# A hybrid attention layer on one core: copies of h on ScalarE, earlier sums, rotated tiles stored ahead of weights

## The chip, the cores and the metric

The kernel runs on one NeuronCore of a Trainium2 chip. The metric is the device time of one execution in microseconds (us), as the median of several executions. The engines are named as the profile names them: PE (TensorE, matrix products), PEld (its weight loads), DVE (VectorE), ACT (ScalarE), POOL (GpSimd) and SP (SyncE, which issues the DMAs here; SPq is its queue).

## What is computed

One layer over x of shape 1024 x 1024, with 256 memory tokens. What matters for the change is the start: the norm, the combined projection, and the rotary turn of queries and keys.

```python
def hybrid_layer(x, mem, g_pre, w_in, w_conv, attn_sink, g_mem, w_mem_kv,
                 w_up_a, w_up_b, w_up_m, w_out, g_post):
    h = rms_norm(x, g_pre)
    proj = h @ w_in                                   # 1024 x 1024 by 1024 x IN_WIDTH
    (a_b, a_c, a_x, a_z, b_q, b_k, b_v, b_z, m_q, m_z, gate_logits) = jnp.split(proj, idx, axis=-1)
    ua = (short_gated_conv(a_b, a_c, a_x, w_conv) * silu(a_z)) @ w_up_a
    q, k = partial_rope(b_q, pos), partial_rope(b_k, pos)
    ub = (window_attention_with_sink(q, k, b_v, attn_sink) * silu(b_z)) @ w_up_b
    mk, mv = jnp.split(rms_norm(mem, g_mem) @ w_mem_kv, 2, axis=-1)
    um = (memory_cross_attention(m_q, mk, mv) * silu(m_z)) @ w_up_m
    merged = gates[0] * ua + gates[1] * ub + gates[2] * um      # sigmoid gates of gate_logits
    return x + rms_norm(merged @ w_out, g_post)
```

## The kernel before

Every fp32 product is made of three fp32r products: each operand is split into a high part (a rounded copy) and a low part (value minus high part), and high·high, high·low and low·high are summed in PSUM. High parts are made by ACT, low parts by POOL or DVE.

The projection is worked off in pairs of 128-column tiles. Weights come in 128x512 blocks (`spots`), and each is split into a ring of four (`high_part`, L1060, on ACT; `low_part`, L657, on POOL). One entry of the ring is a "slot"; slots 0 to 11 are the four blocks A11, A21, A12, A22 of each of the first three pairs, which are multiplied directly (`first_pair` and `direct_pair`). They give the keys, the values and the four query tiles. From pair 3 (`P_DIRECT`) on, seven products by Strassen's scheme replace eight: P1, P2, P6, P7, P4, P5, P3, in that order (slots 12 to 18, then 19 to 25 for pair 4, and so on). They need four combinations of the blocks of h: T1 = B12 - B11, T3 = B22 - B12, T2 = B22 - T1, T4 = B21 - T2, each of four 128x512 pieces. P6 uses T2, P7 T3, P4 T4 and P5 T1, and each combination needs high and low parts again (`high_of_combination` on ACT; `low_of_combination` on DVE, for T1 half on DVE and half on POOL).

h itself is made in the first pair: PE transposes a piece of scaled x into PSUM (`turn_x`, L804), ACT writes the high part times g_pre (`high_of_h`), and DVE's `copy_h` (L1374) makes the low part of piece 0 and of odd pieces, and an fp32 copy of each of the 16 pieces into `area`, from which POOL takes the low parts of the even pieces (`low_of_h`, L663) and DVE the sums. PE may overwrite a PSUM bank with the piece four further on once it has been copied.

The five tiles of keys and queries ("rope tiles", 0 the keys, 1 to 4 queries) are rotated on DVE: `swap_rows` and `times_cos` read PSUM, `rotate` (two instructions, L1517 and L1519) reads SBUF alone. Then ACT writes the high part (`rope_high`, L1127), POOL the low part (`rope_low`, L676), and SP stores both to DRAM (`store_rope`, L394). `times_cos` of tiles 2 and 3 reuses the space of tiles 0 and 1 and so waits for their stores. When all five are rotated, SP copies one strip of the last (`last_queries`), loads the first attention block (`load_block(0)`, L449), and PE scores it ahead of P6 of pair 4.

All five engine programs are written out by hand, and each engine keeps that order: an instruction that waits holds everything behind it. `sums_first` (L1416) makes the first weight sums of a pair from A11, A21 and A22. SP loads A22 of pair 3 once POOL has made the low part of slot 11. These lines show the order on two of the engines:

```python
            high_of_combination(T3)      # ACT, behind high_part(7)
            high_part(8)
            high_of_combination(T2)
            high_part(9)
            rope_high(0)
            high_part(10)
            rope_high(1)
            high_part(11)
            high_of_combination(T4)
```

Of the kernel before, what the change touches and what calls it, by code (L numbers as in the profile page):

```python
# [155 lines left out]
def hybrid_layer(nc, x, mem, w8, wup, wmem, wout, g_pre, g_mem, g_post, w_conv, sink,  # L156
                 cos, sin, mask, ident_in, out):
    ctx = ExitStack()
    with ctx:
# [142 lines left out]
        x_turned, h_copied, comb_hi = sem("x_turned"), sem("h_copied"), sem("comb_hi")  # L302
# [76 lines left out]
        def _(sp):  # L379
# [52 lines left out]
            for j in range(4):  # L432
                load_spot(j, 2)
            load_spot(A11, 3)
            load_spot(A12, 3)
            store_rope(0)
            load_spot(A21, 3)
            load_spot(A22, 3)
            store_rope(1)
# [108 lines left out]
            for p, name in ORDER[N_DIRECT:]:  # L548
# [8 lines left out]
                if name == "P1":  # L557
                    load_spot(A11, p + 1)
                    if p == P_DIRECT:
                        store_rope(2)  # L560
# [12 lines left out]
                elif name == "P6":  # L573
                    load_spot(A22, p + 1)
                    store_block(p - 1, "next P6")
                    if p == P_DIRECT:
                        store_rope(3)
# [6 lines left out]
                elif name == "P7":  # L584
                    store_block(p - 1, "next P7")
                elif name == "P4":
                    if p == P_DIRECT:
                        last_queries()
                        load_block(0)
                        store_rope(4)  # L590
                    if p == P_LAST:
                        load_gate(0)
                elif name == "P5":
                    if 1 <= gr < ATT_GROUPS and gr % 2 == 1:
                        load_sb(gr // 2)
                    if P_CONV <= p < P_LAST:
                        load_mq(p + 1 - P_CONV)
# [59 lines left out]
        def _(pool):  # L657
# [5 lines left out]
            def low_of_h(n):  # L663
                idx, j, place = H_BLOCKS[n]
                pool.wait_ge(h_copied, n + 1)
# [26 lines left out]
            low_part(7)  # L692
            low_part(8)
            low_part(9)
            rope_low(0)
            low_part(10)
            rope_low(1)
            low_part(11)
            low_part(12)
            low_part(13)  # L700
# [3 lines left out]
            rope_low(2)  # L704
            low_part(15)
            low_part(16)
            low_part(17)
            low_part(18)
            rope_low(3)
            low_part(19)  # L710
            rope_low(4)
            for n in range(20, NS + 3):
                low_part(n)
# [11 lines left out]
        def _(pe):  # L725
# [25 lines left out]
            def first_pair():  # L751

                for n in range(2 * KC):
                    half, kk = divmod(n, KC)
                    for m in {5: (), 6: (8,), 7: (9, 10)}.get(n, (n + 3,)):
                        if 4 <= m < 2 * KC:
                            pe.wait_ge(h_copied, m - 3)
# [301 lines left out]
        def _(act):  # L1059
# [26 lines left out]

            def high_of_combination(idx):
# [17 lines left out]
            for n in range(2 * KC):  # L1105
                high_of_h(n)
                if n == 1:
                    square_sum(5)
# [19 lines left out]
            def rope_high(j):  # L1128
                act.wait_ge(roped, j + 1)
                if j == 0:  # L1130
                    act.wait_ge(comb_hi, 2 * HC)
# [5 lines left out]
            high_of_combination(T3)  # L1137
            high_part(8)
            high_of_combination(T2)
            high_part(9)  # L1140
            rope_high(0)
            high_part(10)
            rope_high(1)
            high_part(11)
            high_of_combination(T4)
            high_part(12)
            high_part(13)
            high_of_combination(T1)
            high_part(14)
            rope_high(2)  # L1150
# [3 lines left out]
            nc.scalar.copy(v_raw, tile_bank(V_TILE)).then_inc(v_copied, 1)  # L1154

# [70 lines left out]
            for n, (p, name) in list(enumerate(ORDER))[N_DIRECT:]:  # L1226
# [24 lines left out]
                elif name == "P2":  # L1251
                    if p - 1 in SILU:
                        block_sigmoid(p - 1, 3, c12)
                elif name == "P6":
                    if p == P_DIRECT:
                        rope_high(3)
# [4 lines left out]
                elif name == "P7":  # L1261
                    if p == P_DIRECT:
                        rope_high(4)
# [81 lines left out]
        def _(dve):  # L1345
# [29 lines left out]
            def copy_h(n):  # L1375
# [3 lines left out]
                dve.wait_ge(h_hi_made, n + 1)  # L1379
# [4 lines left out]
                nc.vector.tensor_scalar(f32(place, HALF), spare[n % 4], g, None, ALU.mult).then_inc(h_copied, 1)  # L1384

            def sum_t1(j):
                b11, b12 = f32(B11F + j * HALF, HALF), f32(B12F + j * HALF, HALF)
                dve.wait_ge(h_copied, KC + j + 1)
# [3 lines left out]
            def sum_t3(j):  # L1392
                b22, b12 = f32(B22F + j * HALF, HALF), f32(B12F + j * HALF, HALF)
                dve.wait_ge(h_copied, KC + HC + j + 1)
                nc.vector.tensor_tensor(f32(T3F + j * HALF, HALF), b22, b12, ALU.subtract).then_inc(sum_made[T3], 1)

            def sum_t2(j):
# [3 lines left out]
                if j == 0:  # L1401
                    dve.wait_ge(h_lo_pool, KC - 1)
# [122 lines left out]
            for n in range(2 * KC):  # L1525
# [5 lines left out]
                if n >= KC + HC:  # L1531
                    sum_t1(n - KC - HC)
            swap_rows(0)
            times_cos(0)
            for j in range(HC):
                sum_t3(j)
            for j in range(HC):
                sum_t2(j)
# [19 lines left out]
            rotate(3)  # L1558
            rotate(4)
# [142 lines left out]
            for p, name in ORDER[N_DIRECT:]:  # L1702
# [36 lines left out]
                elif name == "P6":  # L1739
                    add_p6(p)  # L1740
                    if p == P_DIRECT:
                        low_of_combination(T1)
# [219 lines left out]
```

## Time and profile before

| what | us |
|---|---|
| median of three runs | 941.97 |
| lowest and highest of them | 941.80, 942.54 |
| the profiled execution, whole | 942.66 |
| its span on the core | 940.8 |
| PE busy | 915.8 (97%) |
| PEld busy | 768.4 (82%) |
| DVE busy | 619.5 (66%) |
| ACT busy | 422.6 (45%) |
| POOL busy | 378.4 (40%) |

The span runs from the first to the last instruction on the core, and the whole execution is 1.9 us longer. Lines such as L660 are lines of the kernel before. The granted clock of PE is at full speed over nearly all of the span (0.999 of it on average). The page puts 97% of the span as PE busy; which of the remaining stretches can be won, and by what, is read from the waits and the timeline.

### The profile page before, as it was taken

Reading aid. Unit: us, or ns where it says so; the run is one execution under the profiler, and the core shown is the slowest. Engines: PE = TensorE matmul, PEld = TensorE weight load, DVE = VectorE, ACT = ScalarE, POOL = GpSimd, SP = SyncE. Lnnn points to the kernel's source line nnn. Section 1 sums busy time; section 2 is a strip of 40 time slices with the busy share of each in tenths; the row PEclk is TensorE's granted clock in tenths of the full one; section 3 lists DMA queues with packets and bytes.
Section 4 is the critical chain, followed back from the end, with each engine's and each line's share of the span. In section 5 each row is a group of like instructions: output and inputs, shape, how many; then the busy total and the mean of one; then the engine's idle time right before and its main releaser. Section 6 shows DMA issues by size and latency. Waiting matters only on the chain. (4 is left out here: it accounts for less than half of the span.)

```text
span 940.8 us, 12512 instructions
## 1 busy us (share of the span) xinstructions
PE 915.8 (97%) x4360; PEld 768.4 (82%) x4360; DVE 619.5 (66%) x1057; ACT 422.6 (45%) x802; POOL 378.4 (40%) x260
## 2 busy tenths in 40 slices
PE   5999999999999999999999999999999999999997
PEld 4788778888888888888888888888888888888885
DVE  5799966655556666656576278888896367763443
ACT  7434465444445466544462434343443553432211
POOL 2457834444444344444434744444442644300000
PEclk9999999999999999999999999999999999999999
DMA  7242656342424333624253422222222874641222
GB/s 281 85 119 82 168 175 204 103 157 101 157 101 160 110 118 107 194 95 171 100 173 132 146 67 80 84 83 81 79 78 85 320 234 146 224 156 68 90 90 89
DMA packets 81181, 124.43 MB, mean 132 GB/s; under 512 B 7008, under 2 KB 40416, under 8 KB 81120
## 3 DMA queue, kind: packets, MB, share of 16 engines
q1 hardware_dynamic: 81120, 123.65, 39.8%
q8 instruction: 35, 0.57, 0.2%
q14 instruction: 26, 0.21, 0.1%
HBM read 90.46 MB, written 33.55 MB: 132 GB/s over the span
## 5 line engine op out<-in xcount | busy, mean ns | idle before, releaser
L660 POOL TENSOR_TENSOR ring<-spots,ring 128x512 fp32r<-128x512 f32 x218 | 311.9, 1434 | 401.7 <-ACT ring L1063 388.9
L733 PE MATMUL pm<-hc,ring 128*128 128x512 f32 x728 | 286.7, 394 | 2.2 <-POOL ring L660 2.2
L735 PE MATMUL pm<-hc,ring 128*128 128x512 f32 x728 | 284.1, 390 | 0.0
L734 PE MATMUL pm<-hc,ring 128*128 128x512 f32 x728 | 283.7, 390 | 0.0
L1063 ACT ACTIVATE ring<-spots 128x512 fp32r<-128x512 f32 x218 | 136.6, 628 | 260.3 <-PE pm L735 183.8
L733 PEld LDWEIGHTS pm<-hc,ring 128*128 128x128 f32 x728 | 136.8, 188 | 29.3 <-issue 2.5
L735 PEld LDWEIGHTS pm<-hc,ring 128*128 128x128 f32 x728 | 136.6, 188 | 28.9
L734 PEld LDWEIGHTS pm<-hc,ring 128*128 128x128 f32 x728 | 136.8, 188 | 26.8
L1289 ACT ACTIVATE area<-area 128x1024 f32<-128x1024 f32 x24 | 25.5, 1061 | 60.6 <-DMA area<-raw_d 60.6
L1013 PE MATMUL pm<-hc,ring 128*128 128x512 f32 x128 | 49.9, 390 | 0.0
L1014 PE MATMUL pm<-hc,ring 128*128 128x512 f32 x128 | 49.8, 389 | 0.0
L1015 PE MATMUL pm<-hc,ring 128*128 128x512 f32 x128 | 49.8, 389 | 0.0
L1048 PE MATMUL pm<-hc 128*128 128x512 f32 x128 | 49.8, 389 | 0.0
L1049 PE MATMUL pm<-hc 128*128 128x512 f32 x128 | 49.8, 389 | 0.0
L1050 PE MATMUL pm<-hc 128*128 128x512 f32 x128 | 49.8, 389 | 0.0
L1460 DVE TENSOR_TENSOR snaps<-pm,snaps 128x512 f32<-128x512 f32 x26 | 17.9, 689 | 37.6 <-PE pm L735 37.6
L1612 DVE TENSOR_TENSOR area<-pv,area 64x512 f32<-64x512 f32 x16 | 11.0, 689 | 46.4 <-ACT area L1171 46.4
L1177 ACT ACTIVATE area<-area,st 128x384 f32<-128x384 f32 x64 | 38.4, 601 | 0.0
L1068 ACT COPY snaps<-pm 128x512 f32<-128x512 f32 x26 | 15.3, 589 | 48.4 <-PE pm L735 48.4
L1806 DVE TENSOR_TENSOR hc<-spots,hc 128x512 fp32r<-128x512 f32 x16 | 22.7, 1418 | 21.7 <-ACT hc L1303 21.6
L1449 DVE TENSOR_TENSOR area<-pm,snaps 128x512 f32<-128x512 f32 x26 | 18.0, 691 | 25.4 <-PE pm L735 17.4
L1184 ACT ACTIVATE area<-area,st 128x384 f32<-128x384 f32 x64 | 34.2, 606 | 0.2
(206 smaller groups left out, 1617.6 us busy)
## 6 DMA issues: line engine op xcount, KB each, us to landing
spots<-in_w SPq DMA_DIRECT2D x116, 256.0 KB, 3.0
raw_d<-area SPq DMA_DIRECT2D x72, 256.0 KB, 2.0
area<-raw_d SPq DMA_DIRECT2D x24, 512.0 KB, 3.5
area<-in_x SPq DMA_DIRECT2D x16, 512.0 KB, 4.8
spots<-in_wup SPq DMA_DIRECT2D x24, 256.0 KB, 3.9
q_d<-area_r SPq DMA_DIRECT2D x16, 256.0 KB, 4.4
area<-raw_d SPq DMA_DIRECT2D x16, 256.0 KB, 3.2
area<-in_wmem SPq DMA_DIRECT2D x16, 256.0 KB, 2.9
```

Source lines behind the costliest of these rows:

```text
L660: nc.gpsimd.tensor_tensor(ring[:, n % RING, 1, :], operand(n), ring[:, n % RING, 0, :].bitcast(F32), ALU.subtract).then_inc(lo_made, 1)
L733: pe.matmul(bank, hi, moving_hi(k), start=(k == 0), stop=False)
L734: pe.matmul(bank, hi, moving_lo(k), start=False, stop=False)
L735: mm = pe.matmul(bank, lo, moving_hi(k), start=False, stop=(k == HC - 1))
L1013: pe.matmul(dst, hi, y[:, at, 0, cols], start=(begin and c == chunks[0]), stop=False)
L1014: pe.matmul(dst, hi, y[:, at, 1, cols], start=False, stop=False)
L1015: mm = pe.matmul(dst, lo, y[:, at, 0, cols], start=False, stop=(end and c == chunks[-1]))
L1048: pe.matmul(dst, hi, wo[:, k, 0, :], start=(k == 0), stop=False)
L1049: pe.matmul(dst, lo, wo[:, k, 0, :], start=False, stop=False)
L1050: mm = pe.matmul(dst, hi, wo[:, k, 1, :], start=False, stop=(k == KC - 1))
L1063: nc.scalar.activation(ring[:, n % RING, 0, :], operand(n), ACT.Copy).then_inc(hi_made, 1)
L1177: ins = nc.scalar.activation(probs[:, h, :], probs[:, h, :], ACT.Exp, bias=st[:, 3, h:h + 1], accum_out=st[:, 5, h:h + 1])
```

## The change

In the first pair, the second eight fp32 copies of h (pieces 8 to 15) move from DVE to ACT, each right behind the piece's high part; DVE keeps their odd low parts, and waits for ACT's copy before each. DVE makes the pieces of T1 and T3 in turns from piece 13 on, then T2, and only then rotates tile 0. ACT and POOL take `rope_high` and `rope_low` of each tile further ahead among the weight blocks, ACT makes T4's high parts before `high_part(11)`, and DVE makes its half of T1's low parts between `rotate(3)` and `rotate(4)` rather than in P6 of pair 3. SP stores tile 0 ahead of the loads of A11 and A12 of pair 3, tile 1 ahead of A21 and A22, and moves the last loads and stores from P4 of pair 3 to P6. The arithmetic is the same. The diff, without the repeated context:

```diff
@@ sync: loads and stores around the direct pairs
+            store_rope(0)
             load_spot(A11, 3)
             load_spot(A12, 3)
-            store_rope(0)
+            store_rope(1)
             load_spot(A21, 3)
             load_spot(A22, 3)
-            store_rope(1)
+            store_rope(2)
...
                 if name == "P1":
                     load_spot(A11, p + 1)
                     if p == P_DIRECT:
-                        store_rope(2)
+                        store_rope(3)
...
                     load_spot(A22, p + 1)
                     store_block(p - 1, "next P6")
                     if p == P_DIRECT:
-                        store_rope(3)
+                        last_queries()
+                        load_block(0)
+                        store_rope(4)
...
                 elif name == "P4":
-                    if p == P_DIRECT:
-                        last_queries()
-                        load_block(0)
-                        store_rope(4)
@@ gpsimd
-                pool.wait_ge(h_copied, n + 1)
+                if n < KC:
+                    pool.wait_ge(h_copied, n + 1)
+                else:
+                    pool.wait_ge(h_copied_act, n - KC + 1)
...
             low_part(7)
+            rope_low(0)
             low_part(8)
             low_part(9)
-            rope_low(0)
-            low_part(10)
             rope_low(1)
-            low_part(11)
-            low_part(12)
-            low_part(13)
+            for n in range(10, 14):
+                low_part(n)
+            rope_low(2)
             for j in (0, 2):
                 low_of_combination(T1, j)
             low_part(14)
-            rope_low(2)
             low_part(15)
+            rope_low(3)
             low_part(16)
             low_part(17)
-            low_part(18)
-            rope_low(3)
-            low_part(19)
             rope_low(4)
-            for n in range(20, NS + 3):
+            for n in range(18, NS + 3):
                 low_part(n)
@@ tensor, first_pair
-                            pe.wait_ge(h_copied, m - 3)
+                            if m - 4 < KC:
+                                pe.wait_ge(h_copied, m - 3)
+                            else:
+                                pe.wait_ge(h_copied_act, m - 3 - KC)
+                                pe.wait_ge(h_lo_dve, h_lo_count(m - 4, h_lo_dve))
@@ scalar
+            def copy_h(n):
+                nc.scalar.activation(f32(H_BLOCKS[n][2], HALF), spare[n % 4], ACT.Identity,
+                                     scale=gpre[:, n % KC:n % KC + 1]).then_inc(h_copied_act, 1)
...
                 high_of_h(n)
+                if n >= KC:
+                    copy_h(n)
...
                 if j == 0:
-                    act.wait_ge(comb_hi, 2 * HC)
+                    act.wait_ge(sum_made[T2], HC)
+                    act.wait_ge(h_lo_pool, h_lo_count(2 * KC - 1, h_lo_pool))
...
             high_of_combination(T3)
+            rope_high(0)
             high_part(8)
             high_of_combination(T2)
             high_part(9)
-            rope_high(0)
+            rope_high(1)
             high_part(10)
-            rope_high(1)
+            high_of_combination(T4)
             high_part(11)
-            high_of_combination(T4)
             high_part(12)
             high_part(13)
+            rope_high(2)
             high_of_combination(T1)
             high_part(14)
-            rope_high(2)
             high_part(15)
...
             nc.scalar.copy(v_raw, tile_bank(V_TILE)).then_inc(v_copied, 1)
+            rope_high(3)
...
                 elif name == "P2":
+                    if p == P_DIRECT:
+                        rope_high(4)
...
                 elif name == "P6":
-                    if p == P_DIRECT:
-                        rope_high(3)
...
                 elif name == "P7":
-                    if p == P_DIRECT:
-                        rope_high(4)
@@ vector
-                dve.wait_ge(h_hi_made, n + 1)
+                if n < KC:
+                    dve.wait_ge(h_hi_made, n + 1)
+                elif n % 2:
+                    dve.wait_ge(h_copied_act, n - KC + 1)
...
-                nc.vector.tensor_scalar(f32(place, HALF), spare[n % 4], g, None, ALU.mult).then_inc(h_copied, 1)
+                if n < KC:
+                    nc.vector.tensor_scalar(f32(place, HALF), spare[n % 4], g, None, ALU.mult).then_inc(h_copied, 1)
...
-                if n >= KC + HC:
-                    sum_t1(n - KC - HC)
+                if n > KC + HC:
+                    sum_t1(n - KC - HC - 1)
+                    sum_t3(n - KC - HC - 1)
+            sum_t1(HC - 1)
+            sum_t3(HC - 1)
+            for j in range(HC):
+                sum_t2(j)
             swap_rows(0)
             times_cos(0)
-            for j in range(HC):
-                sum_t3(j)
-            for j in range(HC):
-                sum_t2(j)
             rotate(0)
             low_of_combination(T3)
...
             rotate(3)
+            low_of_combination(T1)
             rotate(4)
...
                 elif name == "P6":
                     add_p6(p)
-                    if p == P_DIRECT:
-                        low_of_combination(T1)
```

DVE at the end of the first pair: the copies (L1384), the low parts of h (L1381), the sums of T1 (L1390), T3 (L1395) and T2 (L1403), tile 0 (L1503, L1513, L1517, L1519), and T3's low parts (L1413). Before:

```order
L1390 TENSOR_TENSOR area<-area 128x512
L1381 SCALAR_TENSOR_TENSOR hc<-pv,gpre,hc 128x512
L1384 TENSOR_SCALAR area<-pv,gpre 128x512
L1390 TENSOR_TENSOR area<-area 128x512
L1503 STREAM_SHUFFLE area<-pm 128x1024
L1513 TENSOR_TENSOR area<-pm,area 128x1024
L1395 TENSOR_TENSOR area<-area 128x512 x4
L1403 TENSOR_TENSOR area<-area 128x512 x4
L1517 TENSOR_TENSOR area<-area 128x1024
L1519 TENSOR_TENSOR area<-area 128x1024
L1413 TENSOR_TENSOR hc<-area,hc 128x512 x4
```

The same place after the change, where T1 is L1404, T3 L1409, T2 L1417, and tile 0 L1517 to L1533:

```order
L1393 SCALAR_TENSOR_TENSOR hc<-pv,gpre,hc 128x512
L1404 TENSOR_TENSOR area<-area 128x512
L1409 TENSOR_TENSOR area<-area 128x512
L1404 TENSOR_TENSOR area<-area 128x512
L1409 TENSOR_TENSOR area<-area 128x512
L1417 TENSOR_TENSOR area<-area 128x512 x4
L1517 STREAM_SHUFFLE area<-pm 128x1024
L1527 TENSOR_TENSOR area<-pm,area 128x1024
L1531 TENSOR_TENSOR area<-area 128x1024
L1533 TENSOR_TENSOR area<-area 128x1024
L1427 TENSOR_TENSOR hc<-area,hc 128x512 x4
```

All twelve sums now stand in front of tile 0's swap. POOL from the last low parts of h (L667) to the weight blocks of pair 4; L660 is a weight block, L678 a rope tile, L673 T1. Before:

```order
L667 TENSOR_TENSOR hc<-area,hc 128x512 x6
L660 TENSOR_TENSOR ring<-spots,ring 128x512 x6
L678 TENSOR_TENSOR area_r<-area,area_r 128x1024
L660 TENSOR_TENSOR ring<-spots,ring 128x512
L678 TENSOR_TENSOR area_r<-area,area_r 128x1024
L660 TENSOR_TENSOR ring<-spots,ring 128x512 x3
L673 TENSOR_TENSOR hc<-area,hc 128x512 x2
L660 TENSOR_TENSOR ring<-spots,ring 128x512
L678 TENSOR_TENSOR area_r<-area,area_r 128x1024
L660 TENSOR_TENSOR ring<-spots,ring 128x512 x4
L678 TENSOR_TENSOR area_r<-area,area_r 128x1024
```

The same place after the change, with L659 for a weight block, L680 for a rope tile and L675 for T1:

```order
L669 TENSOR_TENSOR hc<-area,hc 128x512 x6
L659 TENSOR_TENSOR ring<-spots,ring 128x512 x4
L680 TENSOR_TENSOR area_r<-area,area_r 128x1024
L659 TENSOR_TENSOR ring<-spots,ring 128x512 x2
L680 TENSOR_TENSOR area_r<-area,area_r 128x1024
L659 TENSOR_TENSOR ring<-spots,ring 128x512 x4
L680 TENSOR_TENSOR area_r<-area,area_r 128x1024
L675 TENSOR_TENSOR hc<-area,hc 128x512 x2
L659 TENSOR_TENSOR ring<-spots,ring 128x512 x2
L680 TENSOR_TENSOR area_r<-area,area_r 128x1024
L659 TENSOR_TENSOR ring<-spots,ring 128x512 x2
```

Rope tile 2 now stands ahead of T1's low parts and of slot 14, and tile 3 ahead of slot 16.

## Rows read from the trace of the kernel before

**Rows 1.** Waits of PE, whole span: line, releaser, us in total, times, longest.

```profile
PE sa L817 <- DVE area L1371: 11.1, 2, 9.7
PE pm L733 <- POOL ring L660: 2.2, 1, 2.2
PE sa L841 <- DMA area_r<-kl_d: 1.9, 1, 1.9
```

**Rows 2.** Timeline of PE from P6 of pair 3: start, duration, instructions, [idle before, releaser].

```profile
95.59 0.39 PE L733 MATMUL pm<-hc,ring 128*128 128x512 f32 x1
...
101.92 0.39 PE L733 MATMUL pm<-hc,ring 128*128 128x512 f32 x1
...
106.96 0.47 PE L733 MATMUL pm<-hc,ring 128*128 128x512 f32 x1 [2.16 <-POOL ring L660]
...
120.02 0.41 PE L841 MATMUL sa<-area_r 128*128 128x384 f32 x1 [1.92 <-DMA area_r<-kl_d]
```

**Rows 3.** Timeline of DVE, T1's low parts in P6 of pair 3.

```profile
103.57 3.18 DVE L1413 TENSOR_TENSOR hc<-area,hc 128x512 fp32r<-128x512 f32 x2
```

**Rows 4.** Timeline of PE, first pair: the transposes of pieces 13 and 14.

```profile
37.07 0.60 PE L817 MATMUL sa<-ident,area 128*128 128x128 f32 x4
...
38.89 0.60 PE L817 MATMUL sa<-ident,area 128*128 128x128 f32 x4
```

**Rows 5.** Timeline of ACT: high part of piece 13, high parts of T4, rope tile 2.

```profile
37.70 0.69 ACT L1084 ACTIVATE hc<-sa,gpre 128x512 fp32r<-128x512 f32 x1 [1.13 <-PE sa L817]
...
73.69 2.44 ACT L1092 ACTIVATE hc<-area 128x512 fp32r<-128x512 f32 x4 [4.03 <-DVE area L1408]
...
88.03 1.06 ACT L1132 ACTIVATE area_r<-area 128x1024 fp32r<-128x1024 f32 x1 [0.41 <-DVE area L1519]
```

**Rows 6.** Timeline of DVE, first pair and rope tiles 0 to 2.

```profile
33.18 1.40 DVE L1384 TENSOR_SCALAR area<-sa,gpre 128x512 f32<-128x512 f32 x2
...
46.16 0.01 DVE L1503 LOAD_MASK_SELECT area<-pm  x1 [1.51 <-PE pm L749]
...
47.39 1.20 DVE L1513 TENSOR_TENSOR area<-pm,area 128x1024 f32<-128x1024 f32 x1
48.52 3.31 DVE L1395 TENSOR_TENSOR area<-area 128x512 f32<-128x512 f32 x4
...
55.41 2.19 DVE L1519 TENSOR_TENSOR area<-area 128x1024 f32<-128x1024 f32 x1
...
71.83 1.22 DVE L1513 TENSOR_TENSOR area<-sa,area 128x1024 f32<-128x1024 f32 x1 [2.32 <-DMA kl_d<-area_r]
...
75.38 4.90 DVE L1413 TENSOR_TENSOR hc<-area,hc 128x512 fp32r<-128x512 f32 x8
...
83.89 0.69 DVE L1431 TENSOR_TENSOR spots<-spots 128x512 f32<-128x512 f32 x1
...
85.74 2.26 DVE L1519 TENSOR_TENSOR area<-area 128x1024 f32<-128x1024 f32 x1
...
90.49 2.83 DVE L1439 TENSOR_TENSOR spots<-spots 128x512 f32<-128x512 f32 x1
93.24 2.31 DVE L1517 TENSOR_TENSOR area<-area 128x1024 f32<-128x1024 f32 x1
```

**Rows 7.** Timeline of POOL: weight blocks and rope tiles 0, 2 and 4.

```profile
46.92 2.55 POOL L660 TENSOR_TENSOR ring<-spots,ring 128x512 fp32r<-128x512 f32 x2 [1.11 <-ACT ring L1063]
...
59.91 2.84 POOL L678 TENSOR_TENSOR area_r<-area,area_r 128x1024 fp32r<-128x1024 f32 x1
...
90.38 2.39 POOL L678 TENSOR_TENSOR area_r<-area,area_r 128x1024 fp32r<-128x1024 f32 x1
...
106.17 2.84 POOL L678 TENSOR_TENSOR area_r<-area,area_r 128x1024 fp32r<-128x1024 f32 x1
```

**Rows 8.** Timeline of POOL, narrow stretch: slot 12's low part during DVE's run.

```profile
76.73 4.71 POOL L660 TENSOR_TENSOR ring<-spots,ring 128x512 fp32r<-128x512 f32 x1 [3.86 <-ACT ring L1063]
```

**Rows 9.** DMA issues between 68 and 80 us: count, KB each, median us to landing.

```profile
spots<-in_w SPq DMA_DIRECT2D x2, 256.0 KB, 3.5
```

More of the change, by code:

```diff
@@ L301, in hybrid_layer @@
         inv_made, xs_act = sem("inv_made"), sem("xs_act")
-        x_turned, h_copied, comb_hi = sem("x_turned"), sem("h_copied"), sem("comb_hi")
+        x_turned, h_copied, h_copied_act, comb_hi = sem("x_turned"), sem("h_copied"), sem("h_copied_act"), sem("comb_hi")
         h_hi_made, h_lo_pool, h_lo_dve = sem("h_hi_made"), sem("h_lo_pool"), sem("h_lo_dve")
@@ L1383, in copy_h @@
                                                    op1=ALU.subtract).then_inc(h_lo_dve, 1)
-                nc.vector.tensor_scalar(f32(place, HALF), spare[n % 4], g, None, ALU.mult).then_inc(h_copied, 1)
+                if n < KC:
+                    nc.vector.tensor_scalar(f32(place, HALF), spare[n % 4], g, None, ALU.mult).then_inc(h_copied, 1)
             def sum_t1(j):
                 b11, b12 = f32(B11F + j * HALF, HALF), f32(B12F + j * HALF, HALF)
-                dve.wait_ge(h_copied, KC + j + 1)
+                dve.wait_ge(h_copied, j + 1)
+                dve.wait_ge(h_copied_act, j + 1)
                 dve.wait_ge(h_lo_pool, h_lo_count(HC, h_lo_pool))
@@ L1393, in sum_t3 @@
                 b22, b12 = f32(B22F + j * HALF, HALF), f32(B12F + j * HALF, HALF)
-                dve.wait_ge(h_copied, KC + HC + j + 1)
+                dve.wait_ge(h_copied_act, HC + j + 1)
                 nc.vector.tensor_tensor(f32(T3F + j * HALF, HALF), b22, b12, ALU.subtract).then_inc(sum_made[T3], 1)
@@ L1401, in sum_t2 @@
                 if j == 0:
-                    dve.wait_ge(h_lo_pool, KC - 1)
+                    dve.wait_ge(h_lo_pool, h_lo_count(KC + HC - 1, h_lo_pool))
                 nc.vector.tensor_tensor(f32(B12F + j * HALF, HALF), b22, t1, ALU.subtract).then_inc(sum_made[T2], 1)
```

## The prediction

> **What bounds the kernel now.** I read the waits of PE first: the page has PE busy for 97% of the span, so the time is PE's work plus its waits. Three waits matter [rows 1]. The 11.1 us stand at the start, before x is scaled, where the change touches nothing. The other two, 2.2 and 1.9 us, are all that the rotary tiles and the combinations cost PE; the rest of PE's idle time is in pieces below 1.7 us elsewhere. The timeline of PE places them [rows 2]: P6 of pair 3 begins at 95.59, P4 at about 101.9, P5 begins at 106.96 behind a wait of 2.16, and the first scores at 120.02 behind a wait of 1.92. The reader is to see that PE runs without a gap from 30 us to the first of these, and that from 120 us on nothing of this part holds it again. So the change can win at most 2.16 + 1.92 = 4.08 us, and what it wins is decided at four places: P6, P4 and P5 of pair 3, and the first scores.
>
> The releaser named for the first wait, a weight block on POOL, is not the whole of it. P5 needs both halves of T1's low parts, and DVE makes its two in 103.57 to 106.75 [rows 3], after the rotation of all five tiles; P5 starts 0.2 us behind them. The second wait is for the keys' low parts from DRAM: rope tile 4's low part is ready at 106.17 + 2.84 = 109.0 [rows 7], and SP's four small copies, three loads and their landing take the 11.0 us from there to 120.0.
>
> **The first pair.** PE comes to a new piece every 1.82 us (37.07 to 38.89) [rows 4]. An ACT operation on such a piece takes 0.69, with 1.13 idle ahead of it [rows 5]; a second one makes about 1.3 us of work per 1.82, so ACT keeps pace. The last piece needs its low part at 45.3 us and gets it at about 43.9, and piece 14 is ready at 43.3 where PE comes to it at 43.9: cost nothing, cover 0.6 us. DVE loses eight copies of 0.7 us (1.40 for the two at 33.18) [rows 6], but not all is gained: it idles 1.5 us before tile 0's swap today (at 46.16) [rows 6].
>
> **What the work costs that comes after it.** The prices are: a half-size sum or low part on DVE 4.90/8 = 0.6 us and a full-size step of `rotate` 1.2 [rows 6]; on POOL a half-size low part 2.55/2 = 1.27 and a rope tile 2.39 [rows 7]; on ACT 0.6 and 1.06 [rows 5]. DVE and POOL don't run these side by side. At 90.49 one DVE sum takes 2.83 instead of 0.6, since POOL has rope tile 2 until 92.77 [rows 6, 7]; the next step of DVE takes 2.31 instead of 1.2, behind one POOL block; and when DVE is in an unbroken run of pieces (75.38 to 80.28), POOL's block of 1.3 us takes 4.71 [rows 8]. Swap and cosine product, which read PSUM, don't take part: at 47.39 the product takes its 1.20 beside POOL's blocks. So the time of this part is the sum of both engines' SBUF work, and the copies that leave DVE read PSUM and were no part of that sum.
>
> The Trainium skill's page "SBUF — State Buffer", section "SBUF: two separate sides", says that DVE operations with two SBUF inputs and GpSimd operations share one pair of ports under an exclusive lock for the whole instruction, and that ACT has its own. The trace agrees (2.83 for a 0.6 us sum). It speaks against the idea that DVE's and POOL's new order can be counted engine by engine: by the rule the steps add up, as below; without it each engine alone would be done in time and the kernel would gain its 4.08 us.
>
> **The chain after the change, step by step.**
> Step A, tile 0 rotated. Today 55.41 + 2.19 = 57.6. From 43.3 us on there are four weight blocks on POOL (5.1 us) and eight sums on DVE (4.9 us), all ahead of tile 0's swap: 53.3 if all four blocks go between the sums, 50.8 if two fall under swap and product. Swap, product and two steps of `rotate` add 4.8, less what overlaps: 57.8 or 55.4. I take the middle, 56.7.
> Step B, product of tile 2. It waits for tile 0's store. ACT 1.1, POOL's wait for DVE 0.6, POOL 2.4, and from the end of the low part (59.91 + 2.84 = 62.75) to the product (71.83) 9.1 us as today [rows 6, 7]: A + 13.2 = 69.9, against 71.8.
> Step C, tile 2 rotated. DVE's run from the product through T4's low parts takes 71.83 to 80.28 = 8.4. New here: the low part of slot 11 now stands behind T4's high parts (73.69 today, 4 x 0.6 [rows 5]), so POOL asks for it in the middle of DVE's run and, as it did at 76.73 [rows 8], gets it only at the end, 1.3 us later. Only then does SP issue the load of A22, which lands 3.5 us later [rows 9], and 0.3 for the hand-over: 13.5 after B, where DVE has been ready at 10.8. Today that load is long there. Three weight sums 2.0 and `rotate` 2.4: C = B + 17.9 = 87.8, against 85.74 + 2.26 = 88.0. The gain of step B is given back.
> Step D, slot 14 for P6. POOL now has rope tile 2 and T1's two pieces ahead of it: 1.1 + 2.4 + 0.6 + 3 x 1.27 + 2 x 1.2 = 10.3, less 0.5 that the recorded durations overlap: C + 9.8 = 97.6. P6 would start at 95.6: a new wait of 2.0 to 2.1.
> Step E, tile 4's low part. From the start of tile 2's low part (C + 1.1), POOL does 3 tiles and 6 blocks (7.2 + 7.6) and DVE one sum, two rotations and two of T1's pieces (0.6 + 4.8 + 1.2), in turns: 21.4, less 5% for the same overlap (90.38 to 95.55 is 5.2 us for 5.4 of prices [rows 6, 7]) = 20.3. So C + 21.4 = 109.2, against 109.0.
> Step F, scores. 11.0 later: 120.2, against 120.02. SP's loads of A12, A21 and A22 of pair 4 stand ahead of its small copies, but their slots are done by 105: no cost.
>
> The four waits are then: P6 2.1; P4 for slot 16 behind rope tile 3, about 0.9; P3 for slot 18 behind tile 4, 0.4; scores 0.9. Together 4.3, in place of 4.08. P5's wait goes, since DVE's T1 is done near 101.
>
> **Sum.** 4.3 - 4.1 = +0.2 to 0.3 us. Against the profiled execution (span 940.8, whole 942.66) that is 941.1 and 942.9; against the median of 941.97, which lies 0.7 below the profiled one, 942.2. A copy on ACT has no row of its own; its bounds are 0.6 (an ACT half from SBUF) and 0.7 (from PSUM), and both are hidden.
>
> **The rivals.**
> Both waits go, -4.1 us, 937.9. For it speaks that DVE has 5.6 us less work and idles less, and that T1's low parts come ahead of the last rotation; if DVE and POOL fall less into each other than in the rows, C comes early. The scores are free of the load if C + 32.4 is below 115.9, so C at 83.5; at P6, slot 14 wants C at 85.8. Against it: it takes 4.5 us off a chain in which I find 0.2. Halfway, with A at 55.4, slot 11 slipping into DVE's run (C two us earlier) and one POOL block less in D, C is near 85.5 and the gain 2 to 2.5: 939.7. I give 0.13 to the full gain and 0.17 to the part of it that is above 0.2%.
> Slower: the same chain with all turns lost. A at 57.8, the full prices in step E without the 5%, and A22 landing 1 us later because tile 1's stores are still under way: C = 89.9 and E = C + 22.5 = 112.4, scores at 123.4, +3.4, 945.3; with half of that, 943.9. It decides from C = 89.6 on. I give 0.22 to slower by over 0.2%. The mechanism is the one above, POOL's queue holding slots 14 and 16 behind rope tiles; only the size differs.
> The first pair turns slower: if POOL's low part of piece 14 or DVE's of piece 15 comes behind sums that now stand ahead, PE waits up to 0.7 us at 43.9 or 45.3, and most of it is taken back at the scores, which don't wait for PE: 942.4, within "same", chance 0.1 of it.
>
> **How the numbers follow.** A measurement of this kernel can tell about 0.2%, 1.9 us, from no change. Forecast within that: 0.48. Faster: 0.13 + 0.17 = 0.30. Slower: 0.22. The likeliest case alone lies between A at 55.4 and 57.8, that is 940.9 to 943.6. The range goes to both rivals: 937.9, where both waits are gone, to 944.2, leaving out about 0.15 above and little below.
>
> **What would show it.** In the profile of the changed kernel: no wait in the first pair beyond 0.3 us; the product of tile 2 at about 70 us behind a DMA; DVE idle for 2 to 3 us before the weight sums of pair 3, released by the load of spots; `rotate` of tile 2 done near 88; PE waiting about 2 us at P6 for POOL; tile 4's low part near 109; scores near 120. If DVE finds A22 landed and `rotate` of tile 2 ends below 85, step C is wrong and the kernel is faster. If P6 doesn't wait, step D is. If the scores start above 122, the turns between DVE and POOL cost more than their sum, and it is slower.

## The result and the profile after

| what | before | after |
|---|---|---|
| median, us | 942.41 (10 runs) | 944.84 (10 runs) |
| lowest and highest, us | 941.80, 943.58 | 943.44, 945.55 |
| span of the profiled execution, us | 940.8 | 942.9 |
| DVE / ACT / POOL busy, us | 619.5 / 422.6 / 378.4 | 612.6 / 425.8 / 379.9 |

The ratio is 1.0023, with a 95% interval of 1.0015 to 1.0032: the changed kernel is slower by about 2.4 us, where 942.2 had been forecast within 937.9 to 944.2. Line numbers of after differ from those of before by -2 to +16: a product of the pairs is L731 to L733, the scores L843, a weight block on POOL L659, a rope tile L680.

Waits of PE, profile of after (us in total, times, longest), to be held against [rows 1]:

```profile
PE sa L819 <- DVE area L1380: 11.0, 2, 10.1
PE sa L843 <- DVE area_r L1589: 3.1, 1, 3.1
PE pm L731 <- POOL ring L659: 1.6, 3, 1.2
...
PE pm L743 <- issue: 1.0, 1, 1.0
```

P5's wait of 2.16 is gone, as forecast, and three smaller ones stand in its place. But the wait at the scores has grown from 1.92 to 3.07, and **its releaser is another**: not the keys' low parts from DRAM, but L1589 on DVE, the low parts of the values. The timeline of PE in after, which answers to [rows 2] (P6, P4, P3, the scores):

```profile
96.89 0.47 PE L731 MATMUL pm<-hc,ring 128*128 128x512 f32 x1 [1.22 <-POOL ring L659]
...
103.62 0.47 PE L731 MATMUL pm<-hc,ring 128*128 128x512 f32 x1 [0.16 <-POOL ring L659]
...
109.53 0.47 PE L731 MATMUL pm<-hc,ring 128*128 128x512 f32 x1 [0.22 <-POOL ring L659]
...
121.03 0.41 PE L843 MATMUL sa<-area_r 128*128 128x384 f32 x1 [3.07 <-DVE area_r L1589]
```

PE comes to the scores at 121.03 - 3.07 = 117.96, a little earlier than before (120.02 - 1.92 = 118.10), and leaves 1.01 us later. That explains 1.0 of the span's 2.1 us. The rest comes right behind. In windows of 2 us of PE (columns: stretch, its length, busy time and instructions, granted clock, DMA share, GB/s), first after, then before:

```profile
122.00:124.00 2.00, 2.00 (x7) 0.50 0.98 342
124.00:126.00 2.00, 2.00 (x8) 0.67 0.60 228
126.00:128.00 2.00, 2.00 (x11) 1.00 0.35 134
```

```profile
122.00:124.00 2.00, 2.00 (x10) 1.00 0.80 243
124.00:126.00 2.00, 2.00 (x10) 1.00 0.78 235
```

Behind the longer wait PE is granted the 1.2 GHz level for about 3.5 us, and a product of the same shape takes 0.63 instead of 0.39. The next landmark that both traces share, the first transpose of the probabilities, shows what that cost. A product and the first transpose in after, then the same transpose in before:

```profile
123.41 0.63 PE L732 MATMUL pm<-hc,ring 128*128 128x512 f32 x1
...
134.99 0.27 PE L851 MATMUL sa<-ident,area 128*128 128x128 f32 x1
```

```profile
132.50 0.44 PE L849 MATMUL sa<-ident,area 128*128 128x128 f32 x2
```

After is 2.49 us behind there and was 1.01 behind at the scores: **1.48 us are the clock**. The other traces bear this out: from the start of the scores to that transpose PE takes 12.3 to 12.7 us in the seven whose clock is full there (12.48 in before), 13.7 to 14.0 in the five where it is low for about 3.5 us, and 15.2 in the one where it is low for 7. From there on the distance stays (2.43 near 508 us, 2.1 at the end).

Why the values are late is read on SP and DVE. Timeline of SP, after: tile 3's store (L405, L407), three weight loads of pair 4 (L392), the keys' low parts (L462):

```profile
101.27 0.58 SPq L405 DMA_DIRECT2D q_d<-area_r  x1
...
103.54 1.23 SPq L407 DMA_DIRECT2D q_d<-area_r  x1
104.87 2.86 SPq L392 DMA_DIRECT2D spots<-in_w  x3
...
112.09 0.61 SPq L462 DMA_DIRECT2D area_r<-kl_d  x1
```

And the same loads in before, where tile 2's store stood ahead of them:

```profile
95.06 1.23 SPq L407 DMA_DIRECT2D q_d<-area_r  x1
96.39 2.90 SPq L392 DMA_DIRECT2D spots<-in_w  x3
```

The loads of A12, A21 and A22 go out 8.5 us later than before, since the store ahead of them waits for tile 3's low part (ready at 101.2) rather than tile 2's. Timeline of DVE, after, with the first weight sum of pair 4 (L1436) and the last low part of the values:

```profile
106.85 0.69 DVE L1486 TENSOR_TENSOR area<-pm,snaps 128x512 f32<-128x512 f32 x1
111.81 0.99 DVE L1436 TENSOR_TENSOR spots<-spots 128x512 f32<-128x512 f32 x1 [4.27 <-DMA spots<-in_w]
...
120.13 0.75 DVE L1589 TENSOR_TENSOR area_r<-pv,area_r 128x256 fp32r<-128x256 f32 x2
```

DVE stands still for 4.27 us, with everything that it has to do in order behind it, the values too. In before the same low part ends at 118.6, 1.4 us ahead of the scores:

```profile
117.84 0.76 DVE L1573 TENSOR_TENSOR area_r<-pv,area_r 128x256 fp32r<-128x256 f32 x2
```

### The profile page after: what moved, and what is told of

It reads as the page before. It is cut to its first block and busy times, and to the rows that moved or that the text cites. A ratio compares the mean times of both kernels' runs of the same rounds, so it can differ in the third digit from the quotient of the medians.

```text
span 942.9 us, 12512 instructions
## 1 busy us (share of the span) xinstructions
PE 916.7 (97%) x4360; PEld 769.1 (82%) x4360; DVE 612.6 (65%) x1049; ACT 425.8 (45%) x810; POOL 379.9 (40%) x260
## 5 line engine op out<-in xcount | busy, mean ns | idle before, releaser
L659 POOL TENSOR_TENSOR ring<-spots,ring 128x512 fp32r<-128x512 f32 x218 | 312.1, 1436 | 391.8 <-ACT ring L1065 379.3
L731 PE MATMUL pm<-hc,ring 128*128 128x512 f32 x728 | 287.3, 395 | 1.6 <-POOL ring L659 1.6
L733 PE MATMUL pm<-hc,ring 128*128 128x512 f32 x728 | 284.4, 391 | 0.0
L731 PEld LDWEIGHTS pm<-hc,ring 128*128 128x128 f32 x728 | 137.2, 188 | 29.4 <-issue 2.8
L733 PEld LDWEIGHTS pm<-hc,ring 128*128 128x128 f32 x728 | 136.9, 188 | 29.1
L1474 DVE TENSOR_TENSOR snaps<-pm,snaps 128x512 f32<-128x512 f32 x26 | 17.9, 690 | 39.2 <-PE pm L733 39.1
L1820 DVE TENSOR_TENSOR hc<-spots,hc 128x512 fp32r<-128x512 f32 x16 | 24.8, 1551 | 18.0 <-ACT hc L1312 17.9
L1346 ACT ACTIVATE area<-pm 128x1024 f32<-128x1024 f32 x7 | 7.2, 1029 | 58.0 <-PE pm L1052 58.0
```

The source lines that it names most:

```text
L659: nc.gpsimd.tensor_tensor(ring[:, n % RING, 1, :], operand(n), ring[:, n % RING, 0, :].bitcast(F32), ALU.subtract).then_inc(lo_made, 1)
L731: pe.matmul(bank, hi, moving_hi(k), start=(k == 0), stop=False)
L733: mm = pe.matmul(bank, lo, moving_hi(k), start=False, stop=(k == HC - 1))
```

## The experiments

The theory: the late weight loads hold DVE, DVE holds the values, the values hold the scores, and the wait of over 3 us lets the clock fall. The rival: the chain of turns between DVE and POOL, on which the prediction rests, is what costs. Differences of a few tenths between single executions say little; where several runs stand, their ratio to before in the same batch is given.

### The values ahead of the wait

After, with the values made in P7 of pair 3, ahead of the weight sum that waits:

```diff
                 elif name == "P7":
                     add_p7(p)
+                    if p == P_DIRECT:
+                        make_values()
...
-                    if p == P_DIRECT:
-                        make_values()
```

> The changed kernel with one thing moved: DVE makes the attention values (make_values) in step P7 of pair 3, ahead of the weight sums of pair 4, instead of behind them. Theory: in the changed kernel the scores wait for DVE, which waits 4.3 us for the weights of pair 4; with the values made in that idle time the scores wait only for the keys' load, which lands near 119, so they start near 119.1 instead of 121.0, the wait is 1.0 to 1.3 us, PE's clock stays at its full level, and the time falls by 1.9 + 1.5 = 3.4 us, to about 941.4. Rival: the keys' load lands near 121 too, the wait stays near 3 us and the time within 0.5 us of 944.8.

Measured 940.94 (11 runs), ratio to before 0.9987 [0.9979, 0.9996], span 938.7. Timelines of PE and DVE:

```profile
118.69 0.41 PE L843 MATMUL sa<-area_r 128*128 128x384 f32 x1 [0.73 <-DMA area_r<-kl_d]
```

```profile
108.89 0.76 DVE L1589 TENSOR_TENSOR area_r<-pv,area_r 128x256 fp32r<-128x256 f32 x2
...
111.56 0.97 DVE L1436 TENSOR_TENSOR spots<-spots 128x512 f32<-128x512 f32 x1 [1.32 <-DMA spots<-in_w]
```

The values lie in what was DVE's idle time, the scores start 2.34 us earlier, the named releaser is again the keys' DMA, and the clock stays at 2.4 GHz. Against after the median is 3.9 us less (3.4 by the two ratios to before) and the span 4.2: 2.3 from the scores' earlier start, and 1.5 of the clock by the first transpose, at 131.11. The load of A22 lands about as late as in after (the weight sum starts at 111.56), so it isn't the load itself that costs, but what is queued behind it on DVE. This carries most of the explanation.

### The wait made in the kernel before

Before, with four idle copies on DVE ahead of the values, which changes no load and no turn:

```diff
                 dve.wait_ge(v_turned, 2)
+                for _ in range(4):
+                    link(nc.vector.tensor_copy(cosb[:, 0:HALF], sa[:, 2, :]))
```

> The kernel before with four extra copies of 128x512 from PSUM on DVE, into space that is free, right ahead of the values, which makes them about 2.9 us later. It does nothing else. Theory: the scores start near 121.5 and wait 3.3 to 3.6 us in place of 1.92; an idle time of that length at this place takes PE's clock to its lower level for about 3.3 us, as in the changed kernel, which costs another 1.5: 2.8 to 3.2 us over the kernel before. Rival: the clock falls in the changed kernel for the sum of its waits (the one at P6 too), and here it stays: 1.3 to 1.7 us over before.

Measured 944.36 (7 runs, 943.71 to 945.98), ratio 1.0025 [1.0014, 1.0036]; the profiled execution has 943.5 for its span, 2.7 more than before. PE and its windows:

```profile
121.38 0.41 PE L841 MATMUL sa<-area_r 128*128 128x384 f32 x1 [3.57 <-DVE area_r L1575]
```

```profile
122.00:124.00 2.00, 2.00 (x8) 0.51 1.01 245
124.00:126.00 2.00, 2.00 (x7) 0.63 0.94 354
```

Late values alone, in the old order, give the longer wait and the lower clock. The scores start 1.36 us later than in before and the first transpose 2.83 us later, so the profiled execution shows the full price. It is one of the longer ones (945.64): the median is 1.9 above before's and the ratio says 2.4, both between the 1.4 of the late start alone and the 2.8 expected. The seven times stand in two clumps (943.7 to 944.4, 945.6 to 946.0). Whether the clock stays up in the lower one can't be said, since only one execution has windows.

### The loads ahead of tile 3's store

After, with the store of tile 3 behind the loads of A12 and A21:

```diff
                     load_spot(A11, p + 1)
-                    if p == P_DIRECT:
-                        store_rope(3)
...
                     load_spot(A21, p + 1)
+                    if p == P_DIRECT:
+                        store_rope(3)
```

> The changed kernel with SP's loads of A12 and A21 of pair 4 issued ahead of the store of rope tile 3 instead of behind it. Theory: only A22 is left to issue near 104.9, it lands near 109.7 instead of 111.8, DVE's wait for it shrinks from 4.3 to about 2 us, the values are done near 118.8 and the scores start near 119.0, with PE waiting 1 to 1.3 us. Rival: the landing is set by the stores' traffic on the DMA engines rather than by the place in SP's queue; A22 lands at 111 or later and the scores start near 121.

One execution: 942.47, span 940.7. Timelines of DVE and PE:

```profile
109.76 1.44 DVE L1436 TENSOR_TENSOR spots<-spots 128x512 f32<-128x512 f32 x1 [2.21 <-DMA spots<-in_w]
111.23 1.67 DVE L1438 TENSOR_TENSOR spots<-spots 128x512 f32<-128x512 f32 x1
```

```profile
120.40 0.41 PE L843 MATMUL sa<-area_r 128*128 128x384 f32 x1 [2.42 <-DVE area_r L1589]
```

A22, now the only load behind the store and not the third of three, lands 2.05 us earlier, as expected; the store's place is thereby shown as a cause. But the scores gain only 0.63: the sums now run while POOL does its three blocks of 108.1 to 112.4, and two of them take 1.44 and 1.67 instead of 0.7. The clock doesn't fall behind this wait of 2.42. So the span is 2.2 us shorter than after's with the scores only 0.6 earlier: the other 1.6 are the clock (the first transpose, at 132.81, comes 2.18 earlier).

### Copies alone, and order alone

Before, with nothing but ACT's copies of pieces 8 to 15 and the waits that go with them:

```diff
                 high_of_h(n)
+                if n >= KC:
+                    copy_h(n)
...
-                nc.vector.tensor_scalar(f32(place, HALF), spare[n % 4], g, None, ALU.mult).then_inc(h_copied, 1)
+                if n < KC:
+                    nc.vector.tensor_scalar(f32(place, HALF), spare[n % 4], g, None, ALU.mult).then_inc(h_copied, 1)
```

> The kernel before with only the eight copies of h moved from DVE to ACT, and every order as before. Theory: the first pair goes at PE's pace either way, so tile 0's swap still waits for PE at 46.2 us and nothing changes: within 0.4 us of the kernel before. Rival: the copies on ACT delay weight blocks or DVE's low parts of odd pieces, PE waits in the first pair, and part of the 2.4 us loss shows here.

Measured 942.08 (11 runs), ratio 0.9997 [0.9988, 1.0006]: no difference. In its profiled execution P5 waits 2.20 us and the clock falls behind that wait, on PE's windows:

```profile
108.00:110.00 2.00, 2.00 (x7) 0.53 0.94 225
110.00:112.00 2.00, 2.00 (x7) 0.62 0.50 117
```

The scores start at 119.55 without a wait, 0.5 earlier than in before: PE lost about as much by the clock as it would have waited there. A fall costs nothing where a wait lies ahead that takes it up.

After, with the copies back on DVE:

```diff
                 high_of_h(n)
-                if n >= KC:
-                    copy_h(n)
...
-                if n < KC:
-                    nc.vector.tensor_scalar(f32(place, HALF), spare[n % 4], g, None, ALU.mult).then_inc(h_copied, 1)
+                nc.vector.tensor_scalar(f32(place, HALF), spare[n % 4], g, None,
+                                        ALU.mult).then_inc(h_copied if n < KC else h_copied_act, 1)
```

> The changed kernel with the eight copies left on DVE, all orders as changed. Theory: the loss comes from the order of the queues, so it stays: 2 to 4 us over the kernel before, since DVE reaches tile 0 later by up to 1 us. Rival: the loss comes from ACT's copies and is gone here (within 0.5 us of before).

Measured 946.40 (5 runs), ratio 1.0043 [1.0030, 1.0056], 4.0 us over before. The profiled execution is the quickest of the five (945.0). P6 waits 2.29 us instead of 1.22 and the scores 1.95, and the clock is low in two places, behind P6 and behind the scores:

```profile
97.64 0.47 PE L731 MATMUL pm<-hc,ring 128*128 128x512 f32 x1 [2.29 <-POOL ring L659]
```

```profile
98.00:100.00 2.00, 2.00 (x7) 0.60 0.27 97
...
122.00:124.00 2.00, 2.00 (x8) 0.57 0.98 313
124.00:126.00 2.00, 2.00 (x6) 0.57 0.74 283
```

So the new order costs 4.0 us with DVE's copies and 2.4 with ACT's. The copies gain nothing in the old order and about 1.6 us in the new one, where the twelve sums stand ahead of tile 0 (the two intervals just overlap, and a second fall of the clock is part of it).

### T1 ahead of tile 2, slot 11 ahead of T4

After, with T1's parts and slot 14 ahead of rope tile 2, on ACT and on POOL alike; POOL's side of the edit:

```diff
-            rope_low(2)
             for j in (0, 2):
                 low_of_combination(T1, j)
             low_part(14)
+            rope_low(2)
```

> The changed kernel with T1's parts and slot 14 ahead of rope tile 2 on ACT and POOL, as in the kernel before. Theory: the wait at P6 (1.2 us) goes, but the scores still wait for DVE and the weights of pair 4 until about 121, so PE waits 4.2 us or more there and the span stays within 0.6 us of the changed kernel's. Rival: the wait at P6 was on the path and the span falls by 1.2 us or more.

One execution: 944.63, span 942.8 against 942.9. P6 no longer waits, P4 waits 1.73, and the scores 3.60:

```profile
103.66 0.47 PE L731 MATMUL pm<-hc,ring 128*128 128x512 f32 x1 [1.73 <-POOL ring L659]
...
121.12 0.66 PE L843 MATMUL sa<-area_r 128*128 128x384 f32 x1 [3.60 <-DVE area_r L1589]
```

A wait ahead of the scores is only moved, since the values set their start. P6's wait, the longest new one that the prediction named, isn't what made the kernel slower.

After, with the high part of slot 11 ahead of T4's high parts, so that POOL has it before DVE's long run:

```diff
-            high_of_combination(T4)
             high_part(11)
+            high_of_combination(T4)
```

> The changed kernel with the high part of slot 11 made ahead of T4's high parts on ACT, as in the kernel before. Theory: POOL makes slot 11 near 72.5 instead of in DVE's run, A22 of pair 3 lands before 79, DVE does not wait for it (1.47 us less), tile 2 is rotated near 85.5 instead of 87.0, the wait at P6 falls from 1.2 to 0.3 or less, and the scores come near 119.6, 1.4 us earlier. Rival: DVE meets POOL's other blocks instead and tile 2 is rotated at 86.5 or later, with the wait at P6 at 0.8 or more.

One execution: 947.57, span 945.8; my theory didn't hold. DVE doesn't wait for A22 of pair 3 any more, but T4's sums take 3.50 us instead of 2.49, and in this execution POOL's next block gets into DVE's run of T4's low parts. That run, in this kernel and then in after:

```profile
75.09 5.99 DVE L1427 TENSOR_TENSOR hc<-area,hc 128x512 fp32r<-128x512 f32 x8
```

```profile
73.86 4.90 DVE L1427 TENSOR_TENSOR hc<-area,hc 128x512 fp32r<-128x512 f32 x8
```

The order alone doesn't decide this: the kernel of all three edits below has slot 11 in the same place, a run of 4.89, and tile 2 rotated at 86.6. So one execution doesn't price the edit. Here tile 2 is rotated at 87.75 instead of 87.0, the stores and loads follow, and the scores start at 122.15 behind a wait of 3.46. The clock then is low for about 7 us:

```profile
122.00:124.00 2.00, 1.85 (x6) 0.50 0.94 320
124.00:126.00 2.00, 2.00 (x7) 0.50 0.82 300
126.00:128.00 2.00, 2.00 (x6) 0.50 0.03 11
```

### Put together, and better versions

The edits of the values, of tile 3's store and of slot 11 together:

> The changed kernel with three edits together: values in P7 of pair 3, loads of A12 and A21 of pair 4 ahead of tile 3's store, slot 11's high part ahead of T4's. Theory: the scores start near 117.4, limited by PE's own arrival (116.5) and the keys' load, waits of 1.2 us in all, no fall of the clock: about 939.3, 3 us below the kernel before. Rival: what slot 11 gives is lost again in POOL's queue, and the time is that of the changed kernel with early values alone, 940.9.

Measured 941.95 (11 runs, 939.44 to 942.59), ratio 0.9988 [0.9978, 0.9997]. I had expected 939.3; three of the eleven times lie at 939.4 to 940.1, six at 941.9 to 942.6. The profiled execution is one of the six (942.22), and its scores wait for the keys' load:

```profile
119.32 0.41 PE L843 MATMUL sa<-area_r 128*128 128x384 f32 x1 [1.75 <-DMA area_r<-kl_d]
```

That is 0.6 later than with the values alone, though the chain ahead of it is 0.4 earlier: tile 2 is rotated at 86.6, and SP issues the keys' low parts at 111.70 instead of 112.09. From that issue to the scores it takes 7.6 us here and 6.6 with the values alone. Why, isn't shown, nor what the quick executions do, since none of them has a trace. So what the places of slot 11 and of the loads are worth once the values are early stays open.

After with the values early, and the first attention block loaded ahead of the last tile's strip, whose copies SP had ahead of the keys:

```diff
                     if p == P_DIRECT:
-                        last_queries()
                         load_block(0)
+                        last_queries()
                         store_rope(4)
```

> The changed kernel with the values in P7 of pair 3, and SP's loads of the first attention block ahead of the four small copies of the last queries instead of behind them. With early values alone the scores waited 0.73 us for the keys' load (118.69). Theory: the three loads are issued 1.5 to 2.4 us earlier, land before PE arrives, the wait of 0.7 us goes or becomes one for the small copies of 0.3 us at most, and the time is 0.4 to 0.7 us below early values alone, near 940.3. Rival: the block's loads and the copies share the DMA engines, the last of them lands as late as before, and the time is that of early values alone.

Measured 940.03 (6 runs), ratio 0.9968 [0.9956, 0.9980]: the lowest median, 2.8 us under before and 4.8 under after. Against the values alone the gain isn't shown in the same way: the intervals overlap a little, and both profiled executions have a span of 938.7. The keys' low parts are issued at 110.01 instead of 112.09, and PE doesn't wait at the scores:

```profile
118.12 0.33 PE L843 MATMUL sa<-area_r 128*128 128x384 f32 x1
```

The same with T1 and slot 14 ahead of tile 2, the edit shown above:

> The same with T1's parts and slot 14 ahead of rope tile 2 on ACT and POOL as well. Theory: the wait at P6 (1.2 us) goes, one of 1.7 us at P4 takes its place as it did with that edit alone, so nothing is gained: within 0.6 us of the kernel with values and block loads early. Rival: with the scores no longer held, what P6 gains arrives at the end: 1.2 us less.

Measured 940.47 (6 runs), ratio 0.9971 [0.9959, 0.9982]. P6's wait is gone and P4's is 1.70: nothing gained, the blocks are only taken in another order. That points to POOL's work up to slot 16 as what bounds PE there; no run takes a block of it away.

### After once more

> The changed kernel itself, once more, beside the two others. Theory: a wait of about 3 us at the scores, PE's clock at its lower level for 3 us or more right behind it, and 2 to 3 us over the kernel before. Rival: the fall of the clock was a chance of the one profiled execution; it stays at full level here, and the profiled span is 1 us over that of the kernel before.

Measured 944.84 (11 runs), ratio 1.0019 [1.0010, 1.0028]. The scores wait 3.26 us and the clock is 0.50 behind them, so neither was a chance of one execution. Both series of after have one run with a mean clock of 0.999, and it is the fastest of its series (943.44 and 943.33), 1.4 to 1.5 us under the median; the other runs have 0.997 or less. That would fit with a fall that stays out now and then, but those runs have no windows, and the mean clock alone says little: of the 55 runs of before beside the experiments, 27 have 0.996 or 0.997 and 18 have 0.999, with nearly the same mean time (942.5 and 942.6). The profiled execution of before is one of those with 0.999. Where the clock falls in the others isn't recorded; the trace of the copies alone, whose mean is 0.997 too, shows one place where a fall costs nothing.

## Why the prediction was wrong, step by step

- **First pair: right.** No new wait beyond the noise of the issue (1.0 us against 0.3, a place where executions of these kernels differ by up to 1.3; the second execution of after has none). A copy on ACT takes 0.68; the bounds were 0.6 and 0.7.
- **Steps A to C: right to a microsecond.** Tile 0 is rotated at 57.1 (56.7 forecast), tile 2's product starts at 70.3 (69.9), and DVE waits for A22 and has tile 2 rotated at 87.0 (87.8). The low part of slot 11 was held up by DVE's run as forecast, until 79.9. Step C by itself took 16.7 us after B, not 17.9: A22 landed 2.5 us after its issue where 3.5 had been put, and DVE waited 1.47 instead of 2 to 3. These are the lines of after on POOL and DVE that answer to [rows 6] and [rows 8]; the first holds three blocks, slot 11's among them:

```profile
75.21 7.21 POOL L659 TENSOR_TENSOR ring<-spots,ring 128x512 fp32r<-128x512 f32 x3 [3.86 <-ACT ring L1065]
```

```profile
82.59 0.69 DVE L1436 TENSOR_TENSOR spots<-spots 128x512 f32<-128x512 f32 x1 [1.47 <-DMA spots<-in_w]
...
85.78 1.22 DVE L1533 TENSOR_TENSOR area<-area 128x1024 f32<-128x1024 f32 x1
```

- **Steps D and E: right in themselves, 0.8 us early with step C.** P6 starts 9.9 us behind C (9.8 forecast), and tile 4's low part is ready at 108.1, 21.1 behind C (21.4 forecast). So P6 waits 1.22 for POOL where 2.1 had been put, and nearly all of the difference is C's 0.8. P3 waits 0.22 (0.4). P4 waits 0.16 where 0.9 had been put, a figure for which the prediction shows no working. Tile 4's row answers to [rows 7]:

```profile
105.73 2.41 POOL L680 TENSOR_TENSOR area_r<-area,area_r 128x1024 fp32r<-128x1024 f32 x1
```

  The turns behind these steps held: sums of 0.7 us take 1.44 and 1.67 beside POOL's blocks, and T4's run grows from 4.90 to 5.99 where one block gets in. The page "SBUF — State Buffer" of the Trainium skill says in "SBUF: two separate sides" that the one that comes later is blocked for the other's whole instruction, and these figures agree.
- **Step F: this failed.** It said that the loads of A12, A21 and A22 of pair 4 stand ahead of SP's small copies, "but their slots are done by 105: no cost". The first half was right: SP issued them at 104.87, and the keys' DMAs went out on time. What I didn't ask is who needs what these loads bring. DVE wants the weights at 107.5 for its first sum, gets them at 111.81, and has the values behind that sum. Moving the store of tile 3 from P6 to P1 put it ahead of three loads, and I priced the store's move for the queue's own later entries only, not for the consumers of the loads on another engine. The step's term was 0.9 us for the scores' wait; it measured 3.07. With the values early it measured 0.73.
- **A missing term: the clock.** The sum had no price for what PE does after a wait; it measured 1.48 us in after. The row with which I could have bounded it was there: PE had two waits of about 2 us in before and ran on at full clock, and nothing showed what a longer one does.
- **The sum.** Forecast +0.2 to 0.3. Measured in the spans +2.1: waits +0.6 (4.67 against 4.08), gaps too small for an entry and the first pair +0.4, the clock +1.5, less 0.4 by the end. Had the scores started at 118.7, as with the values early, the kernel would have come out 1.5 us under before in the median. That is 0.16%, within what the forecast called no difference. Two smaller figures of the forecast don't follow from its terms: half of the slower rival's 3.4 over 941.97 is 943.7 and not 943.9, and A at 57.8 instead of 56.7 gives 943.3 and not 943.6.
- **The rivals.** Slower was the outcome, but not by the mechanism that I gave it. Its price came from lost turns, with step C later than 89.6; C was at 87.0. The gain of both waits wasn't reached by any version; the nearest, after with the values early and the first block's loads ahead, has 940.03.

What stays open: whether the low clock alone accounts for the difference between the clumps of times with the late values, why those with all three edits spread over 3 us, and why P4 waits so little.

## What to carry to other kernels

When a transfer that waits is moved ahead of others in a queue, list every later entry of that queue and, for each, the engine that needs what it brings and the work queued behind that need: the cost appeared two hops away, in values that have nothing to do with the weights. Work that another engine awaits belongs ahead of a wait that it doesn't need: moving `make_values` up was worth 3.4 to 3.9 us with no instruction changed. And a wait of PE of over 3 us was dearer here than its length, since the clock fell behind it; a row on the granted clock after each of the longest waits belongs to the reading.

## What the runs showed that I had not expected

The granted clock of PE after a single wait. Behind waits of 3.07, 3.26, 3.46, 3.57 and 3.60 us at the scores it went to the 1.2 GHz level in all five traces, for some 3.5 us, and cost 1.2 to 1.5 us from the scores to the first transpose; behind 3.46 it stayed low for 7 us and cost 2.7. Behind waits of 1.95, 2.20 and 2.29 us it fell too (order alone at two places, copies alone at one). Behind 1.92, 2.16, 2.21 and 2.42 us it did not (both waits of before, P5's wait with the late values, the loads first), and behind 1.75 us or less never. The 10 us ahead of PE's first work aren't counted. So from 1.95 to 2.42 us the length of the wait doesn't decide it alone, and what else does isn't settled by these runs.
